# Last attention on tiles of 32 tokens by four heads, with turns on VectorE and through memory

## What is computed

```python
def swa_sinks(q, k, v, sinks):          # q: 256 x 32 x 64, k and v: 256 x 4 x 64, blocks of 128 tokens
    ...
    scores = jnp.einsum('bnihgd,bnjhd->bnhgij', qb, kk).astype(jnp.float32) * (d ** -0.5)
    band = (kj <= qi) & (qi - kj < WINDOW)
    scores = jnp.where(valid[None, :, None, None], scores, -1e30)
    m = jnp.maximum(jnp.max(scores, axis=-1, keepdims=True), sink)
    p = jnp.exp(scores - m)
    p = p / (jnp.sum(p, axis=-1, keepdims=True) + jnp.exp(sink - m))
    o = jnp.einsum('bnhgij,bnjhd->bnihgd', p.astype(v.dtype), vv)

def odd_mixer(h, w_in, q_norm_w, k_norm_w, sinks, w_out, pos):
    ...
    q = rope(rms_norm_2(q.reshape(b, s, ATTN_Q_HEADS, ATTN_HEAD_DIM), q_norm_w), pos)
    k = rope(rms_norm_2(k.reshape(b, s, ATTN_KV_HEADS, ATTN_HEAD_DIM), k_norm_w), pos)
    v = v.reshape(b, s, ATTN_KV_HEADS, ATTN_HEAD_DIM)
    o = swa_sinks(q, k, v, sinks).reshape(b, s, ATTN_WIDTH)
    return (o * jax.nn.silu(gate)) @ w_out
```

## Time and profile before

| what | us |
|---|---|
| median of 3 executions (1879.96 to 1880.33) | 1880.02 |
| the profiled execution | 1879.77 |
| its span, first to last instruction | 1878.0 |
| TensorE busy | 1872.9 |
| VectorE busy | 1246.1 |
| ScalarE busy | 991.1 |

### The profile page before, as it was taken

How to read it: one execution, slowest core, us unless ns; L and a number is a source line. 1 busy time by engine, 2 the same in 40 slices (tenths; PEclk the granted TensorE clock), 3 DMA queues, 4 the chain that set the end, 5 groups by cost and what they waited for, 6 DMA issues and landing times.

```text
span 1878.0 us, 22471 instructions
## 1 busy us (share of the span) xinstructions
PE 1872.9 (100%) x8531; PEld 1543.7 (82%) x8531; DVE 1246.1 (66%) x1861; ACT 991.1 (53%) x1370; POOL 37.6 (2%) x88
## 2 busy tenths in 40 slices
PE   9999999999999999999999999999999999999999
PEld 7888888888888888888888888888888888877777
DVE  6676566776666556665466776765776666777775
ACT  6677554554444344443444455564565555466653
POOL 0001000000000000000000000000000000111100
PEclk9999999999999999999999999999999999999999
DMA  9767764786666666666666696666666677655665
GB/s 324 205 194 179 207 181 152 217 254 196 192 193 194 194 192 191 192 198 192 191 196 195 204 281 196 194 191 190 190 200 194 194 238 235 174 174 175 182 196 171
DMA packets 212363, 375.97 MB, mean 200 GB/s; under 512 B 14672, under 2 KB 35968, under 8 KB 212256
## 3 DMA queue, kind: packets, MB, share of 16 engines
q1 hardware_dynamic: 211008, 371.78, 65.9%
q0 software_dynamic: 816, 2.11, 0.8%
q10 hardware_dynamic: 432, 0.66, 0.1%
HBM read 361.89 MB, written 12.60 MB: 199 GB/s over the span
## 4 chain that ended last, share of the span: by engine, by line
PE 99%; DMA 0%; SPq 0%; DVE 0%; ACT 0%; DVEq 0%; issue 0%
PE g L1225 32%; PE g L1227 32%; PE g L1226 32%; PE m L1159 1%; PE ob L1304 0%; PE m L1286 0%; DMA raw<-in_w_in 0%; PE m L1386 0%; PE m L1284 0%; PE ob L1307 0%; PE m L1271 0%; PE ob L1372 0%; PE m L1316 0%; PE m L1337 0%; PE g L1213 0%; PE g L1212 0%
## 5 line engine op out<-in xcount | busy, mean ns | idle before, releaser
L1696 DVE TENSOR_TENSOR wl<-raw,wh 128x1024 fp32r<-128x1024 f32 (+1 forms) x660 | 802.6, 1217 | 552.7 <-ACT wh L1416 549.4
L1416 ACT ACTIVATE wh<-raw 128x1024 fp32r<-128x1024 f32 (+1 forms) x661 | 695.3, 1053 | 730.9 <-PE g L1227 724.3
L1225 PE MATMUL g<-wh,xh 128*128 128x512 f32 x1886 | 741.1, 393 | 0.3 <-DVE wl L1696 0.3
L1227 PE MATMUL g<-wh,xl 128*128 128x512 f32 x1886 | 734.4, 389 | 0.0
L1226 PE MATMUL g<-wl,xh 128*128 128x512 f32 x1886 | 734.1, 389 | 0.0
L1225 PEld LDWEIGHTS g<-wh,xh 128*128 128x128 f32 x1886 | 354.1, 188 | 78.5 <-issue 3.9
L1227 PEld LDWEIGHTS g<-wh,xl 128*128 128x128 f32 x1886 | 354.0, 188 | 74.0
L1226 PEld LDWEIGHTS g<-wl,xh 128*128 128x128 f32 x1886 | 354.2, 188 | 71.9
L1225 PE MATMUL g<-wh,mh 128*128 128x512 f32 x732 | 287.1, 392 | 0.0
L1227 PE MATMUL g<-wh,ml 128*128 128x512 f32 x732 | 285.0, 389 | 0.0
L1226 PE MATMUL g<-wl,mh 128*128 128x512 f32 x732 | 284.9, 389 | 0.0
(11 more groups left out here) (193 smaller groups left out, 769.5 us busy)
## 6 DMA issues: line engine op xcount, KB each, us to landing
raw<-in_ev_w_in SPq DMA_DIRECT2D x128, 512.0 KB, 3.9
raw<-in_w_in SPq DMA_DIRECT2D x92, 512.0 KB, 4.2
raw<-in_w_gate SPq DMA_DIRECT2D x88, 512.0 KB, 4.4
raw<-in_w_up SPq DMA_DIRECT2D x88, 512.0 KB, 4.3
raw<-in_w_down SPq DMA_DIRECT2D x88, 512.0 KB, 4.6
raw<-in_od_w_in SPq DMA_DIRECT2D x72, 512.0 KB, 4.0
raw<-in_w_out SPq DMA_DIRECT2D x32, 512.0 KB, 4.2
raw<-in_ev_w_out SPq DMA_DIRECT2D x32, 512.0 KB, 4.7
```

The costliest lines, as they stand in the source:

```text
L1225: e.matmul(o, hi[:, kt, c], h, start=first, stop=False)
L1227: last = e.matmul(o, lo[:, kt, c], h, start=False, stop=end)
L1416: return e.activation(o, i, AF.Copy, scale=scale)
L1696: return e.tensor_tensor(o, a, b, op)
```

## The change

A tile of scores is now 32 tokens by four heads on the 128 partitions, with the two heads of a parity pair in two banks. For each j the 128 tokens of a half fall into four chunks of 32; group g takes the chunks 0 and 3 (g even) or 1 and 2 (g odd) of both token halves and of all eight heads, so that both groups of a j are needed for any of its four contraction tiles. Chunk c of the first half meets its 32c + 32 causal keys, and chunk c of the second half the 160 keys from 32c. The transposes on TensorE of queries and probabilities, their copies by ScalarE and VectorE's masks of turned probabilities go; the keys' transposes stay. Queries (`qturn`) and probabilities (`pturn`) are turned in 32x32 blocks by VectorE, sent to memory in one DMA (`qsend`, `psend`) and fetched in four (`qfetch`, `pfetch`), one for each of the four places on the partitions; the roots make the same way (`rsend`, `rfetch`). VectorE adds the mask while it empties the banks (`oadd`), then takes the maximum and scales it (`omax`). ScalarE scales the probabilities by the reciprocal sums (`onrm`) before they are turned, so the gate is turned and sent unweighted, directly after its evacuation. `oapv` works on six slots of 128 columns of turned probabilities; its bank is copied to `AW` in two parts (`oout`); the product with the gate (`mmul`) follows when both groups of a j are there. GpSimd zeroes the two places of turned probabilities once. Added work may now be said with up to 4.5 us queued ahead on VectorE, where it was 1.0 to 2.0. In M5, tiles 0 to 3 of the first two blocks come before 4 to 7, and 8 to 11 of the second half's first two before 12 to 15. The diff, cut to its core:

```diff
...
-    for acts, n in (("X1", 12), ("M3", 8), ("X2", 12), ("X3", 12), ("M5", 14)):
+    for acts, n in (("X1", 12), ("M3", 8), ("X2", 12), ("X3", 12), ("M5", 4), ("M5", 12)):
...
+CHUNKS = ((0, 3), (1, 2))
+TURNED = (((0, 5), (2, 5), (2, 5), (2, 6)), ((0, 4), (0, 5), (2, 6), (4, 6)))
...
+        self.say("qsend", j, k)
+        yield 4
+        self.say("qfetch", j, k)
+        self.end[("qfetch", j, k)] = self.now + 6.5
...
+        self.say("rsend", j)
+        yield 4
+        self.say("rfetch", j)
+        self.end[("rfetch", j)] = self.now + 6.0
...
+        self.say("psend", g)
+        self.end[("psend", g)] = self.now + 5.0
+        yield 4
+        while g >= 2 and ("oapv", g - 2) not in self.said:
+            yield 1
+        self.say("pfetch", g)
+        self.end[("pfetch", g)] = self.now + 8.5
...
+        while ("qfetch", g // 2, 1) not in self.said or g and ("oqk", g - 1) not in self.said:
+            yield 1
+        for _ in range(12):
+            if (all(self.end.get(p, 1e9) <= self.now for p in [("qfetch", g // 2, 1)] + self.ring[-3:][:2]) and
+                    self.through["dve"] - self.now <= 4.5):
+                break
+            yield 1
         say("oqk", g)
-        yield 1
-        yield from self.made("oqk", g)
-        yield from self.room("dve", 1.0)
+        for n in range(2):
+            yield 1
+            yield from self.room("dve", 4.5)
+            say("oadd", g, n)
+        while ("rfetch", g // 2) not in self.said:
+            yield 1
...
+        self.spawn(self.probs_back(g))
+        while ("pfetch", g) not in self.said:
+            yield 1
+        for _ in range(12):
+            if self.end[("pfetch", g)] <= self.now:
+                break
+            yield 1
+        for q in (g // 2 * 2 - 2, g // 2 * 2 - 1):
...
-                        for o, q, k in heads:
-                            e.matmul(o[:, 0:128], q[:, 0:128], k[:, 0:128], start=True, stop=True)
-                        for n, (o, q, k) in enumerate(heads):
-                            e.matmul(o[:, 128:384], q[:, 128:256], k[:, 0:256], start=True,
-                                     stop=True).then_inc(s_pv if i + n == 3 else s_bank, 1)
...
-                    four(lambda c: bank(*p)[:, 128 * c:128 * c + 128],
-                         lambda c: od_probs(g)[:, tiles[c][0], 128 * tiles[c][1]:128 * tiles[c][1] + 128]).then_inc(s_bank, 1)
+                    for n in range(2):
+                        on.wait_ge(*bank_free(*p, n))
+                    for i, c, at, own, end in od_chunks(g):
+                        for k, lo, hi, key in ((0, at, own, 0), (1, own, end, 32 * c)):
+                            for n in range(2):
+                                last = e.matmul(bank(*p, n)[:, lo:hi], qo[rows_of(n), j % 2, k, c, :],
+                                                ko[rows_of(n), j, key:key + hi - lo], start=True, stop=True)
+                                if i and k:
+                                    last.then_inc(s_bank, 1)
...
-                    on.wait_ge(s_masked, nth("oapt", g, 1))
+                    on.wait_ge(s_pback[g % 2], 64 * (g // 2 + 1))
...
-                    for i in (0, 2):
-                        for n in (i, i + 1):
-                            e.matmul(OB[rows_of(n), 128 * i:128 * i + 256], v[:, 0, :], od_turned(n)[0],
-                                     start=True, stop=False, skip_group_check=True)
-                        for n in (i, i + 1):
-                            last = e.matmul(OB[rows_of(n), 128 * i + 128:128 * i + 256], v[:, 1, :], od_turned(n)[1],
-                                            start=False, stop=True, skip_group_check=True)
-                    last.then_inc(s_pv, 1)
+                    for k, t, first, last, slots in ((0, 0, True, True, (0, 2)), (1, 0, True, False, (4, 5)),
+                                                     (1, 1, False, True, (1, 3))):
+                        for n in range(2):
+                            done = e.matmul(OB[rows_of(n), 256 * k:256 * k + 256], v[:, t, :], od_slots(g, n, *slots),
+                                            start=first, stop=last, skip_group_check=True)
+                    done.then_inc(s_pv, 1)
...
+                    for n in range(2):
+                        for kb, lo, hi in ((0, at, own), (1, own, end)):
+                            z = od_probs(g)[:, n, lo:hi]
+                            last = copy(z, z, ri[:, 4 * g + 2 * i + n, kb:kb + 1])
+                    last.then_inc(s_onrm, 1)
...
+                    for i, c, at, own, end in od_chunks(g):
+                        last = tt(od_probs(g)[:, n, at:end], bank("oqk", g, n)[:, at:end], C("band", 96 - 32 * c, 288),
+                                  ALU.add)
+                    last.then_inc(s_bank_dve, 1)
...
+                    for i, c, at, own, end in od_chunks(g):
+                        for kb, lo, hi in ((0, at, own), (1, own, end)):
+                            last = reduce(mx[:, 4 * g + 2 * i:4 * g + 2 * i + 2, kb:kb + 1], od_probs(g)[:, :, lo:hi],
+                                          ALU.max, True)
+                    on.wait_ge(*steps.mark(last))
+                    on.wait_ge(s_rback, 64 * (j + 1))
+                    on.wait_ge(*steps.mark(tt(m, m, od_scale(g), ALU.mult)))
+                    on.wait_ge(*steps.mark(tt(m, m, od_sink(nsink, j), ALU.min)))
+                    tt(by_chunk(es, g), m, od_sink(C("sink"), j), ALU.add).then_inc(s_omax, 1)
...
+                    for c in range(2):
+                        last = tt(tokens(both[:, c]), tokens(both[:, c]), read_back(q, c), ALU.mult)
+                    last.then_inc(s_oprod, 1)
...
+                    for slot, n0, n1, lo in ((2 * i, 0, c + 1, at), (4 + i, c, 4, own), (2 * i + 1, 0, c + 1, end - 32 * c - 32)):
+                        last = e.transpose(probs_own[:, slot + step * n0:slot + step * (n1 - 1) + 1:step],
+                                           od_probs(g)[:, :, lo:lo + 32 * (n1 - n0)].rearrange("p e (b n) -> p b e n", n=32))
+                    last.then_inc(s_pturn, 1)
...
+                    e.transpose(queries_own[k].rearrange("p i m n -> p m i n"),
+                                T3[:, k, 0:512].rearrange("p (m i n) -> p m i n", i=4, n=32)).then_inc(s_qturn, 1)
...
+                    for i in range(4):
+                        e.dma_start(qo[32 * i:32 * i + 32, j % 2, k], queries_there[k].rearrange("(c x) w -> x c w", c=4)
+                                    [:, :, 128 * i:128 * i + 128]).then_inc(s_qback[k], 16)
...
+                    for i, (lo, hi) in enumerate(TURNED[g % 2]):
+                        at = 64 * (3 + g % 2) * i
+                        e.dma_start(probs_turned[g % 2][32 * i:32 * i + 32, :, 64 * lo:64 * hi],
+                                    probs_there[g % 2].rearrange("(m x) w -> x m w", m=4)[:, :, at + 64 * lo:at + 64 * hi]
+                                    ).then_inc(s_pback[g % 2], 16)
...
```

More of the change, by code:

```diff
@@ L178, in say @@
             act, dve = 2.06, 0
+        if p[0] in ("on_sq", "on_sum") and p[1] != "k":
+            act, dve = act / 2, dve / 2
         self.now += pe
-        if p[0] in ("cut", "oapt", "cg", "hmix", "xturn", "mix", "cmix", "xsplit", "xsent", "msent"):
+        if p[0] in ("cut", "cg", "hmix", "xturn", "mix", "cmix", "xsplit", "xsent", "msent"):
             self.work("act", act)
@@ L197, in say @@
             self.norms += 1
-        if p[0] in ("oqk", "oapv"):
+        if p[0] == "oout":
             self.ob = p
-        if p[0] in ("oq_turn", "oapt", "oqk"):
-            self.ring += [p] * (3 if p[0] == "oqk" else 1)
+        if p[0] == "oqk":
+            self.ring += [("oadd", p[1], n) for n in range(2)]
         if p[0] in EMPTIED_BY_ACT + EMPTIED_BY_DVE:
@@ L225, in free @@
         for _ in range(6):
-            if all(self.end[p] <= self.now for p in self.ring[-3:][:n]):
+            if all(self.end.get(p, 1e9) <= self.now for p in self.ring[-3:][:n]):
                 break
@@ L527, in od_quad @@
         yield from self.made("omax", g)
[L528 to L539, removed]
-            yield 1
-        yield from self.made(*self.ob)
-        say("oapv", g)
[L544 to L550, removed]
+        for a in range(2):
+            yield from self.room("act", 3)
+            say("oexp", g, 2 * a)
+            say("oexp", g, 2 * a + 1)
+            yield 1
+        for a in range(2):
+            yield from self.made("oexp", g, 2 * a + 1)
+            yield from self.room("dve", 4.5)
+            say("orec", g, a)
+            yield 1
+            yield from self.made("orec", g, a)
+            yield from self.room("act", 3)
+            say("onrm", g, a)
+        for a in range(2):
+            yield from self.made("onrm", g, a)
+            while g and (("psend", g - 1) not in self.said or self.end[("psend", g - 1)] > self.now):
+                yield 1
+            yield from self.room("dve", 4.5)
+            say("pturn", g, a)
```

(28 more changed lines are left out.)

431 lines of the change are left out of this document (252 added, 179 removed).

## The result

The changed kernel takes 1888.63 us (median of 4 runs, 1887.55 to 1890.78), the kernel before 1880.06 beside it: a ratio of 1.0048, 95% interval 1.0035 to 1.0060. The forecast was 1867.5 us in a range of 1863.5 to 1880; the time lies 21 us above the one and 8.6 above the end of the other.

The account below looks back on a forecast made before the run. TensorE, busy 1872.9 of 1878.0 us, was taken to bound the kernel. From 1879.8 us, 14.3 us less TensorE work plus 2 us of added waits gave 1867.5 us, range 1863.5 to 1880.

Parts of the forecast that it names:

- What bounds the kernel, and the sum on TensorE: Last attention: TensorE work removed shortens the span one for one; transposes -11.1, queries and keys -3.2, sum -14.3 us.
- the third rival: Product of probabilities and values: strided reads cost double, +10.3 us, giving 1875.8 us; chance 0.06.
- The engines beside it: Last attention: VectorE at 82% against 76%, ScalarE some +8 us, 71% against 63%; both keep up on average.
- rival two: VectorE's backlog makes weight cuts 2.0 us late once a group, 16 us: 1881.5, or 1873.5 at half; chance 0.12.
- Memory: Last attention: 12.5 MB more in some 211 us, 59 GB/s on top of 189; the bandwidth is there.
- The added waits: TensorE's new waits for queries and probabilities fetched back in the last attention: 2 us for all, low bound 0.
- unless SP runs late: Condition on queries (4.7 us against 6.5) and probabilities (up to 6.7 against 8.5) arriving inside the plan's margin.
- the first rival: TensorE waits for probabilities at eight products, up to 4.8 us each: 1904, at half 1884.7; chance 0.20, 0.12 slower.
- A waiting TensorE lets SP catch up: Argument against late probabilities in the last attention: SP's lag behind VectorE shrinks while TensorE waits; no size given.
- The price of a wait: TensorE's new waits in the last attention entered the sum at their own length, 2 us in all.
- Twenty-odd us of cover: Last product: last queries' way takes 73 us, ready at 1791, needed near 1817, so nothing is late.
- The ring order of the Trainium skill: DMA engines serve an issuer's descriptors in order; one weight load ahead costs 0.7 us a product, 5.6 us in sum.

Follow-up runs that it names:

- e5: Changed kernel with the sends and fetches of both queries and probabilities issued by GpSimd instead of SyncE: 1873.50 us, 0.9966 of the kernel before.
- e4: Changed kernel with only the queries' sends and fetches issued by GpSimd instead of SyncE: 1875.69 us, 0.9977 of the kernel before.
- e10: Kernel before the change, with TensorE made to wait for GpSimd memsets at 11 places in the feed-forward stage: span 1916.4 us in one execution.
- e2: Changed kernel with 12 needless large matmuls before TensorE's wait for queries at each pair of groups, 48 in all: 1886.19 us, 1.0035 of the kernel before.
- e1: Changed kernel with the plan's time between issue of the queries' fetch and their product raised from 6.5 to 12 us: 1885.28 us, 1.0029 of the kernel before.
- e8: Queries' and probabilities' DMAs on GpSimd; an intended exchange in its order changed nothing, so a repeat of that kernel: 1874.32 us, 0.9969 of the kernel before.

## Why the prediction was wrong, point by point

- **What bounds the kernel, and the sum on TensorE: right.** In e5 the stretch from 1607.7 us takes 259.26 us against 266.55 before, with 5.06 of waits and 0.9 in waits under 0.4 us: TensorE's own work is 13.3 less. I had 14.3. A product of queries and keys costs 1.28 us between large matmuls, 1.39 with the slow start of the next (predicted 1.25 to 1.41), a product of probabilities 1.53 and 1.64 by the same count (1.68): the strided operand costs nothing, the third rival falls.
- **The engines beside it: right.** VectorE's total is 1241.8 us against 1246.1, ScalarE's 1002.2 against 991.1 (I had +8). TensorE waits 1.6 us for wl in the changed kernel; rival two is no cause.
- **Memory: right in size** (12.4 MB more), and the share of 1.03 at 1680 to 1700 us is no cause: e4 has 0.95 there and 1.00 in the next window, and hardly waits for queries.
- **"The added waits": the step that failed.** I set 4.7 us for the queries (four issues and a median landing) against a margin of 6.5, both counted from the issue of the fetch. But that margin starts at the plan's time for the fetch, and SyncE issued it late: turn to fetch took 11 to 15 us where GpSimd, with little ahead, takes 5.5 to 6.5. I counted four issues, the fetch's own; 15 to 20 stand ahead of it behind the turn, 7.5 to 8.8 us, and the waits for wl come on top. I had named the condition ("unless SP runs late") and had the row, SyncE's waits for wl up to 5.5 us, but used it for the first rival alone and for the probabilities. The mechanism of that rival was the right one, at the wrong product: it struck the queries, four times, not the probabilities, eight times.
- **"A waiting TensorE lets SP catch up": no help.** The lateness is no backlog that is carried along; it comes anew between turn and fetch, 11 to 15 us at each of the four places, and TensorE's wait begins only after it. In the last wait, 1776.7 to 1781.2 us, SyncE first issues the late fetch itself.
- **The price of a wait: a missing term.** I counted a microsecond of waiting as one. In e10 each wait of 3.09 to 4.77 us costs another 1.6 to 2.6 us in clock; in the changed kernel three of the four cost 6.2 us together, and e2, which fills them, has these back.
- **"Twenty-odd us of cover" at the end: too much.** In e1, with the queries planned 5.5 us later, the last product waits twice for ml, 5.2 us. In the changed kernel the last parts of ml end at 1847.93, 122 us after the last queries begin to leave PSUM (1725.69), where I had counted 73; in e5, without waits for queries, it is 117. The matmul that waited for them in e1 starts here at 1849.58, some 2 us behind:

```profile
1846.64 1.29 DVE L1802 TENSOR_TENSOR ml<-AW,mh 128x512 fp32r<-128x512 f32 x2
```

```profile
1849.58 0.39 PE L1345 MATMUL g<-wh,mh 128*128 128x512 f32 x1
```

Where the other 44 us or more of this way lie was not worked out.

With the measured terms the sum is 1879.8 - 13.3 + 13.3 + 6.2 + 1.6 = 1887.6; the profiled span of 1885.7 with the 1.8 around it that the execution before had makes 1887.5.

The ring order of the Trainium skill (DMA: Bandwidth & Descriptors, Queues, rings and completion order) would have cost 0.7 us at each product of probabilities by my estimate; these waits are 0.2 us in all.

## What to carry to other kernels

Count the way of a transfer from the moment its data are ready, not from its issue: list everything that its issuing engine does in order between, what each issue costs (0.4 to 0.5 us here) and what each waits for. When a new way through memory is added to a queue whose loads wait for buffers, put it on an engine with little else in its order (here GpSimd: 12.9 us for the queries, 1873 us with the probabilities, faster than both kernels). A longer margin, or moving the roots or the probabilities alone off the queue, only shifted the waits (1885 to 1896 us); easing or moving the loads got back 6 to 8 us. And price a wait of TensorE with what its clock loses after it.

## What was not expected of the hardware

In e10 a wait of TensorE of up to 2.75 us leaves its clock alone, one of 3.09 to 4.77 us is followed by large matmuls 0.43 us apart, and the dearest of those tried was not the longest (2.6 us on top after 3.43, 1.6 after 4.77). The boundary is not sharp: in the changed kernel 2.64 us was enough, and in e5 a wait of 3.14 us was followed by a product at full pace (1.52 us), while in its repeat e8 one of 3.05 us at the same place was followed by a slow one (2.83 us). Why, stays open.
